# Two heads' rotary columns side by side, and the two halves of a state increment in turn, in a two-layer hybrid diffusion block

## The reference

```python
# linear attention: one chunk of 64 tokens, forward and backward in time
o = att @ vc + qe @ S
S = exp(b_last) * S + kd.T @ vc                       # state increment
# latent attention: 128 plain and 64 rotary columns a head, one rotary key for all heads
s = einsum('bqhd,bkhd->bhqk', qn, kn) + einsum('bqhr,bkr->bhqk', qr, kr)
p = softmax(s * scale)
# rotary: latent tokens only; context tokens are not turned
[x1 * cos - x2 * sin, x1 * sin + x2 * cos]            # for the row half, then the column half
```

## Time and profile before

| | |
|---|---|
| median of 3 runs | 3628.59 us (3622.22 to 3632.53) |
| profiled execution | 3628.67 us, span 3626.7 us |
| TensorE busy | 2893.2 us, 80% of the span |
| VectorE, ScalarE, GpSimd busy | 1752.5, 1114.6, 842.5 us |
| DMA | 1071.77 MB, 805.36 of them gathers |
| granted TensorE clock, mean | 0.886 |

### The profile page before, as it was taken

One profiled execution on the slowest core, in us unless ns is written; L12 is line 12 of the kernel. 1 busy time (PEld: TensorE's weight loads), 2 busy tenths in 40 slices (PEclk: granted clock), 3 DMA queues, 4 the chain that ended last, 5 costly groups with the idle time before them and its releaser, 6 DMA issues.

```text
span 3626.7 us, 42720 instructions
## 1 busy us (share of the span) xinstructions
PE 2893.2 (80%) x16338; PEld 1812.9 (50%) x16338; DVE 1752.5 (48%) x4345; ACT 1114.6 (31%) x3086; POOL 842.5 (23%) x772
## 2 busy tenths in 40 slices
PE   7899998888998999988765655599999875565555
PEld 5677887554555666564421111177888751111111
DVE  1323012447666565544766666413300246666764
ACT  1322102243555454324422223232310123222232
POOL 0000000223333333212334434200000023444442
PEclk9999999989999999998987777789999987767766
DMA  8554442788998999977899999731244279999996
GB/s 313 232 201 170 151 151 82 312 312 324 366 365 330 421 420 419 377 269 269 354 364 411 399 419 412 314 116 59 81 151 151 73 306 408 417 411 405 417 396 272
DMA packets 151107, 1071.77 MB, mean 296 GB/s; under 512 B 16564, under 2 KB 18228, under 8 KB 22520
## 3 DMA queue, kind: packets, MB, share of 16 engines
q0 software_dynamic: 110592, 805.36, 55.4%
q1 hardware_dynamic: 40312, 263.69, 19.2%
HBM read 1067.93 MB, written 1.05 MB: 295 GB/s over the span
## 4 chain that ended last, share of the span: by engine, by line
PE 53%; DMA 27%; DVE 9%; ACT 7%; issue 3%; POOL 2%; DVEq 0%; ACTq 0%; SPq 0%; POOLq 0%
PE bank L372 40%; DMA ring<-in_experts,eid 23%; PE bank L386 10%; DVE ring L1317 4%; DMA weights<-in_quads 3%; POOL ring L1734 2%; PE bank L465 1%; ACT topk_work L872 1%; ACT topk_work L865 1%; ACT topk_work L862 1%; ACT L862 0%; PE bank L399 0%; ACT h_even L925 0%; DVE state L1498 0%; ACT L956 0%
## 5 line engine op out<-in xcount | busy, mean ns | idle before, releaser
L1734 POOL DMA_INDIRECT ring<-in_experts,eid x768 | 842.3, 1097 | 2744.9 <-PE bank L386 1416.1
L386 PE MATMUL bank<-ring,topk_work 64*64 64x512 f32 x6144 | 979.4, 766 | 541.4 <-ACT topk_work L872 533.3
L1317 DVE CUSTOM_DVE_ANT_0 ring<-ring,h2tok 128x1024 f32<-128x1024 f32 x768 | 936.6, 1224 | 561.7 <-DMA ring<-in_experts,eid 557.9
L386 PEld LDWEIGHTS bank<-ring,topk_work 64*64 64x64 f32 x6144 | 236.1, 158 | 1191.2 <-ACT topk_work L872 895.4
L862 ACT ACTIVATE topk_work<-topk_work 128x2 f32<-128x2 f32 x384 | 77.9, 203 | 1141.3 <-DVE topk_work L1317 1140.6
L372 PE MATMUL bank<-h_even,weights 128*128 128x256 f32 (+1 forms) x1168 | 279.6, 400 | 40.7 <-DMA weights<-in_quads 26.6
L372 PEld LDWEIGHTS bank<-h_even,weights 128*128 128x128 f32 (+1 forms) x1168 | 224.2, 194 | 100.8 <-DMA weights<-in_quads 28.7
L872 ACT ACTIVATE topk_work<-const,topk_work 128x64 f32<-128x64 f32 x768 | 225.6, 341 | 0.7 <-ACT topk_work L865 0.7
L372 PE MATMUL bank<-h_odd,weights 128*128 128x256 f32 (+1 forms) x896 | 208.4, 389 | 12.7 <-DMA weights<-in_quads 10.3
L372 PE MATMUL bank<-h_even,ring 128*128 128x256 f32 (+1 forms) x896 | 200.0, 382 | 5.3 <-ACT h_even L925 4.7
L372 PEld LDWEIGHTS bank<-h_odd,weights 128*128 128x128 f32 (+1 forms) x896 | 167.3, 190 | 64.1 <-issue 24.2
(11 more groups left out here) (217 smaller groups left out, 3236.7 us busy)
## 6 DMA issues: line engine op xcount, KB each, us to landing
weights<-in_quads SPq DMA_DIRECT2D x137, 1024.0 KB, 8.8
ring<-in_quads SPq DMA_DIRECT2D x98, 1024.0 KB, 4.8
ring<-in_experts,eid POOLq DMA_INDIRECT x768, 9.0
weights<-in_quads SPq DMA_DIRECT2D x7, 768.0 KB, 7.3
ring<-in_quads SPq DMA_DIRECT2D x5, 768.0 KB, 6.5
weights<-in_quads SPq DMA_DIRECT2D x12, 256.0 KB, 2.8
xT<-in_xT SPq DMA_DIRECT2D x1, 2048.0 KB, 11.1
out<-h_even SPq DMA_DIRECT2D x1, 1024.0 KB, 4.5
```

The source lines that it names most:

```text
L386: x = nc.tensor.matmul(acc[g][out, :], diag[mine, J % 4, :], ring[mine, J % RING, D + h * 512:D + (h + 1) * 512], start=first, stop=J % TI ...
L1317: v.tensor_tensor_reduce(row, row, h2tok[:, u // UNITS % 2, :], 1.0, 0.0, ALU.mult, ALU.add, dots[:, u % 2, j:j + 1]).then_inc(S["dot_done ...
L1734: pool.indirect_dma_start(ring[:, J % RING, :], None, d["experts"], bass.IndirectOffsetOnAxis(eid[:, u % 2, j:j + 1], 0)).then_inc(gathere ...
```

## The change

Three things change.

1. The rotary weights are laid out as 64 columns of head 0, 64 of head 1 and so on (quad 0), and the swapped columns of all heads behind them (quad 1). A projection's 128 partitions hold two heads. For latent tokens VectorE multiplies the plain ones by cosines, the swapped ones by signed sines (`turns`) and adds the two in SBUF, a new step `("turned", n, c)`. For context tokens quad 1 is neither loaded nor projected, and the eviction is a copy. The rotary score product is 64 rows deep, from partitions 0 to 63 for even heads and 64 to 127 for odd ones.
2. `scores` takes two units: plain products of both, each in its bank, then both rotary products. It is called before even units only.
3. The increments of a head are issued for the first chunk and then for the second, before the next head.

```diff
-                    for m in range(2):
-                        for g in range(2):
-                            b = job("s", n, u, m, g)
-                            for h in (2 * g, 2 * g + 1):
-                                x = mm(b[:, (h % 2) * DV:(h % 2) * DV + DV], gla_buf(u, GD)[halves[m], h, :],
+                    for g in range(2):
+                        into = [job("s", n, u, m, g) for m in range(2)]
+                        for h in (2 * g, 2 * g + 1):
+                            for m in range(2):
+                                x = mm(into[m][:, (h % 2) * DV:(h % 2) * DV + DV], gla_buf(u, GD)[halves[m], h, :],
                                        Btok[halves[m], t, h * DV:h * DV + DV], True, True)
-                            full(x, "s", n, u, m, g)
+                                if h % 2:
+                                    full(x, "s", n, u, m, g)
...
-                def scores(m):
-                    t, h = au[m]
+                def scores(first):
+
+                    pair = []
+                    for m in (first, first + 1):
+                        t, h = au[m]
+                        if t == 0:
+                            for name in ("qn", "kn"):
+                                pe.wait_ge(*at("evicted", name, n, h))
+                        b = job("sc", n, m)
+                        mm(b[:, 0:TS], A[:, h, tokl(t)], KNc[:, h, :], True, False, skip_group_check=True)
+                        if s:
+                            mm(b[:, TS:2 * TS], A[:, h, tokl(t)], KNl[:, h, :], False, False, skip_group_check=True)
+                        pair.append((m, t, h, b))
                     if t == 0:
-                        for name in ("qn", "qr", "kn"):
-                            pe.wait_ge(*at("evicted", name, n, h))
-                    b = job("sc", n, m)
-                    mm(b[:, 0:TS], A[:, h, tokl(t)], KNc[:, h, :], True, False, skip_group_check=True)
-                    if s:
-                        mm(b[:, TS:2 * TS], A[:, h, tokl(t)], KNl[:, h, :], False, False, skip_group_check=True)
-                    x = mm(b[:, 0:nk * P], B[:, h, tokl(t)], KR[:, 0:nk * P], False, True, skip_group_check=True)
-                    full(x, "sc", n, m)
+                        pe.wait_ge(*(at("turned", n, h // 2) if s else at("evicted", "qr", n, h // 2)))
+                    for m, t, h, b in pair:
+                        mine = slice(h % 2 * ROPE, (h % 2 + 1) * ROPE)
+                        x = mm(b[:, 0:nk * P], B[mine, h // 2, tokl(t)], KR[mine, 0:nk * P], False, True,
+                               skip_group_check=True)
+                        full(x, "sc", n, m)
...
                 scores(0)
-                scores(1)
                 for m in range(len(au) + 1):
-                    if m + 2 < len(au):
+                    if m % 2 == 0 and m + 2 < len(au):
                         scores(m + 2)
...
-                    for name in ("qn", "qr"):
-                        for q in range(2):
+                    for name, count in (("qn", 2), ("qr", 1 + s)):
+                        for q in range(count):
...
-                        v.tensor_tensor(KR[:, span(s)], b[:, 0:TS], cs[:, span(s)], ALU.mult).then_inc(
-                            *mark(DVE_EV, ("evicted", "kr", n, 0)))
+                        if s:
+                            for m in range(2):
+                                mine = slice(m * ROPE, (m + 1) * ROPE)
+                                x = v.tensor_tensor(KR[mine, span(s)], b[mine, 0:TS], turns[mine, m, :], ALU.mult)
+                        else:
+                            x = v.tensor_scalar(KR[:, span(s)], b[:, 0:TS], upper, None, ALU.mult)
+                        x.then_inc(*mark(DVE_EV, ("evicted", "kr", n, 0)))
...
-                    for h in range(MLA_H):
-                        b = bank_of("qr", n, h)
-                        v.tensor_tensor(B[:, h, :], b[:, 0:TS], cs[:, span(s)], ALU.mult).then_inc(
-                            *mark(DVE_EV, ("evicted", "qr", n, h)))
+                    for c in range(4 + 4 * s):
+                        b = bank_of("qr", n, c)
+                        if s:
+                            x = v.tensor_tensor(B[:, c, :], b[:, 0:TS], turns[:, c // 4, :], ALU.mult)
+                            x.then_inc(*mark(DVE_EV, ("evicted", "qr", n, c)))
+                        else:
+                            copy_out(B[:, c, :], b[:, 0:TS], "qr", n, c)
+                    if s:
+                        for c in range(4):
+                            dve.wait_ge(*at("evicted", "qr", n, 4 + c))
+                            v.tensor_tensor(B[:, c, :], B[:, c, :], B[:, 4 + c, :], ALU.add).then_inc(
+                                *mark("dve_step", ("turned", n, c)))
...
-        uqr = np.concatenate([uq[..., NOPE:], uq[..., NOPE:][..., swap]], -1).reshape(QR, -1)
+        uqr = np.concatenate([uq[..., NOPE:].reshape(QR, -1), uq[..., NOPE:][..., swap].reshape(QR, -1)], 1)
```

More of the change, by code:

```diff
@@ L209, in build @@
         dup = const[:, C_DUP:C_DUP + P]
-        cs = const[:, C_CS:C_CS + T]
+        turns = const[:, C_CS:C_CS + 2 * TS].rearrange("p (n t) -> p n t", n=2)
+        upper = const[:, C_TRI + ROPE - 1:C_TRI + ROPE]
         iota16 = const[:, C_IOTA:C_IOTA + 16]
@@ L1777, in constants @@
     t = np.arange(T_LAT)
-    cs = np.zeros((P, T), np.float32)
-    cs[0:ROPE, 0:T_CTX] = 1.0
+    turns = np.zeros((P, 2, TS), np.float32)
     for part, coord in enumerate((t // GRID_W, t % GRID_W)):
@@ L1782, in constants @@
         co, si = np.cos(ang), np.sin(ang)
[L1783 to L1786, removed]
+        for head in range(2):
+            a = head * ROPE + part * half
+            turns[a:a + 16, 0], turns[a + 16:a + 32, 0] = co, co
+            turns[a:a + 16, 1], turns[a + 16:a + 32, 1] = -si, si
+    out[:, C_CS:C_CS + 2 * TS] = turns.reshape(P, -1)
     out[:, C_IOTA:C_IOTA + 16] = np.arange(16)
```

## The result

The change makes the kernel slower: 3706.37 us median (3703.76 to 3709.91) against 3625.4 beside it, a ratio of 1.0226 (95% interval 1.0208 to 1.0243), +81 us. The forecast was 3662 (3638 to 3692), so the sign is right and the time outside the range. The profiled execution has a span of 3707.9 us, 81.2 more than the earlier trace rows.

What follows compares the result with a forecast made beforehand. No single limit: TensorE holds 53% of the chain, DMA 27%. Pass 0 +8.5, pass 1 +9, pass 2 0 and pass 3 +16.2, together +34 us on 3628.7, gave 3662 us, range 3638 to 3692.

Steps and rivals of the forecast that it cites:

- The two waits in attention: Pair order: waits of 1.1 us before odd turns, 1.6 for a score bank; +13 us in pass 3, +10.5 in pass 0.
- shapes: Attention: each score pair switches array shape twice, +0.4 us a pair, +3.2 us in each of passes 0 and 3.
- Rotary halves: Scores: two products on separate array halves run together, 0.86 us off a pair in pass 3, 0.43 in pass 0.
- increments: State records shrink from 2.96 to 1.9 us, but waiting takes the saving: 0 in passes 0, 2, 3; -1 in pass 1.
- projections: Queries: pass 0 drops 24 of 48 records, -5.2 us; the added work in passes 1 and 3 is covered, 0.
- the sum: All passes: pass 0 +8.5, pass 1 +9, pass 2 0, pass 3 +16.2, together +34 us.
- the rival "clock": Attention of passes 0 and 3: new waits lower TensorE's clock for half of both, +30 us, 3692; chance 0.14.
- I take +10: Pass 1's attention: new waits among expert rows cost +10 us, between 0 or -6.9 at best and +30 at worst.
- My sign of being wrong: Wrong if pass 1's attention moves by much more or less than 10 us; other signs were pair length and clock.

Runs made afterwards that it cites:

- experiment 5: The change, with odd units' scores of passes 0 and 3 in the two idle `acc` banks: 3672.03 us, 1.0146 to the kernel before.
- experiment 1: The change, with scores one unit at a time again, 64-row rotary products kept: 3625.0 us, 1.0015 to the kernel before.
- experiment 3: The kernel before, with only the two halves of a state increment in turn: 1.0006 to the kernel before.
- experiment 4: The change, with at most two row pairs in the stretch ahead of pass 1's queries: 3691.18 us, 1.0192 to the kernel before.
- experiment 6: The change, with single scores in pass 1 only, pairs kept in passes 0 and 3: 3658.62 us, 1.0102 to the kernel before.
- experiment 8: The change, with single scores and two half-zero keys, so rotary products keep 128 rows: 3622.62 us, 0.9994 to the kernel before.
- experiment 7: The change, with unread filler products before each new wait in pass 0's attention: 3696.38 us, 1.0202 to the kernel before.
- experiment 11: The kernel before, with three row pairs kept out of pass 1's attention and eight run ahead of its queries: 1.0053 to the kernel before.
- experiment 2: The kernel before, with the pair order alone, rotary products still over 128 rows: 3700.98 us, 1.0218 to the kernel before.

## Why the prediction was wrong

**The two waits in attention: right, in place and nearly in size.** Pass 3 was to lose 13 us and 3.2 for shapes; it lost 16.9, with 8.77 us a pair against 8.3 plus 0.4. The waits are 0.98 and 1.40 where 1.1 and 1.6 stood, and experiment 5 shows that the one for the bank decides. "TensorEngine Tiling (Array Packing)", § Key Properties, of the Trainium skill has changes of mode drain the engine. The traces agree that a change costs time, 0.17 us here (experiment 1); that a drain makes it, they do not show.

**Rotary halves, increments, projections: right.** Two rotary products of 512 columns take 1.06 us together, part of the switches included, against twice the 0.86 of one in the earlier trace rows; "TensorE: Matmul & The Clock Gate", § Part 3 of the Trainium skill, has products on different row groups run at once, and the trace agrees. The increments are worth nothing (experiment 3). Projections were worth 5.2 by the sum. The trace of the change has 6.7 at the first score pair, but those of experiments 1, 4, 5, 6 and 8, with the same projections, have 4.3 to 5.1, and kernels with the old ones differ there by up to 0.9 from one another: the 6.7 is partly that of one execution.

**Pass 0's clock: priced at nothing, and it cost 10 us.** This was the rival "clock", with 0.14, in one attention of the two that it named. The last pairs of the change run at 1.2 GHz. Time line of TensorE at one of them: four records of the rotary pair go out in 1.15 us (341.72 to 342.87), more than the same number of 512 columns takes in pass 3 (1.06), though these have 256. The granted clock in 333 to 347 was 0.50.

```profile
340.56 1.22 PE L373 MATMUL bank<-kn_ctx,ab 128*128 128x256 f32 x2 [1.10 <-ACT gla_work L1116]
...
341.72 1.23 PE L373 MATMUL bank<-krope,ab 64*128 64x256 f32 x4
342.87 0.69 PE L596 MATMUL bank<-const,gla_work 128*128 128x128 f32 x2
```

The change's own trace has pairs at both levels: 5.90 us from the odd turn at 316.21 to the one at 322.11, at a granted clock of 1.00, and 8.20 from 337.06 to 345.26, at 0.50. With the fall pass 0's attention costs 23.2; at a full clock, by experiment 7, 13.3, and the sum had 10.5 + 3.2 = 13.7. I had let waits of 1 to 1.6 us weigh against a fall. They did not keep it up here: no wait in this attention is longer than 1.27 us. In the first 7.2 us, at the end of which the clock first fell (0.96 on the mean), TensorE was busy for 70% (window above). In pass 3's attention it was busy for 73%, with waits of up to 1.7 us, and its clock stayed at 1.00. Neither the length of a wait nor these shares tell the two apart, and why the one fell and the other not stays open.

**Pass 1: the term that failed.** "I take +10" stood for waits in attention among rows, and with -1 for the increments pass 1 had +9. From its first score pair to the first key scores of its queries it lost 46.6. The term was sized as a length of the attention alone, and by that it looks right, +7.5, but this is luck: two larger numbers of opposite sign, as shown below. My sign of being wrong, attention moving by much more or less than 10 us, looked at that length too and could not see it. What the step left out is that the planner decides from the order how many row pairs stand beside attention. A pair of scores and then a short step of 1 us does not give its cost model the same openings, and three row pairs fewer stand there: 12 instead of 15 among TensorE's products, 22 dot products instead of 28 on VectorE in the same stretch. Behind it the kernel remains three to four pairs late through the whole merge. Then comes `breathe(8.0)`: its test compares the next landing with a clock that each pair taken moves on, and with landings 5.0 apart in the plan it does not stop before the limit. In the plan of the kernel before, the third landing stood 7.5 behind the second, and it stopped there. It took two pairs before and takes nine now, 56.1 us at half-idle TensorE (53% busy, window above), waiting 24.8 us for row weights. This is the wait list of that stretch in the changed kernel:

```profile
PE bank L387 <- ACT topk_work L882: 24.8, 6, 8.9
```

Split by the runs: placing rows so without the pair order (experiment 11) gives +14.4 from the first score pair to the first key scores, the change +46.6. The other 32 us are, by subtraction, those of the order in attention, with some 3 for the shapes: the order alone, in experiment 2, loses 43 over the same stretch. At like rows its attention is 7.5 + 14.5 = 22 us longer, hidden in the +7.5 because three pairs' work had left it. The last 10 were not taken apart; for about half of the merge a fourth pair is late in the change, where experiment 11 has three or two. Taking the order out of pass 1 gives 48 us back (experiment 6). Its clock, 0.84 against 0.98, is part of the 22; how much was not tried.

So of the 47 us that the forecast missed (81 against 34) some 38 are pass 1's, 10 pass 0's clock, and the rest near nothing. The two experiments that undo the loss in separate places, 5 in passes 0 and 3 and 6 in pass 1, take back 34 and 48 us, together all of it.

## What to carry to other kernels

Before reordering a software pipeline, write down for each job which job last held its bank: here two scores side by side in a ring of six made one wait for the other's exponential. In pass 3 that cost 2 us a pair, while the halves of the array it was done for gave back 0.9. Where a static planner places other work by modelled time, run the planner on the new order and compare the positions first: here an attention longer by 7.5 us left nine row pairs for a bare stretch that had held two. And an engine's saving counts only as far as the next engine's step behind it: the alternating increments took a third off that step of TensorE and nothing off the kernel.

## What was not expected of the hardware

TensorE's granted clock fell to 0.50 in an attention whose waits were no longer than 1.3 us each; in another, with waits of up to 1.7 us, it stayed at 1.00. Adding sixteen fillers of 0.86 us to the first, 14 us of useless products, kept the clock at 1.00 and made that attention 9.9 us shorter. A switch of the array between 128 and 64 rows cost 0.17 us, 0.34 for there and back. Done for each of 16 units, that is the 5.0 us by which pass 3's attention grew in experiment 1, about as much as the saved projections gave.
